# Thirty-two transposes of the identity on TensorE at two places where it waits

## The reference: what is computed

```python
hn = rmsnorm(h_res, norm1_g[l])
proj = hn @ w_in[l]                                  # 1024 x 3072, six groups of 512 columns
qa, ka, va, qb, kb, vb = jnp.split(proj, splits, axis=-1)
...                                                  # two kinds of attention, oa and ob
mix = jnp.concatenate([oa, ob], axis=-1)
h_res = h_res + mix @ w_out[l]
h_res = h_res + peer(rmsnorm(h_res, norm2_g[l]), peer_wq[l], peer_keys[l], peer_u[l], peer_v[l])
```

## Time and profile before

| | us |
|---|---|
| median of 3 runs | 3197.56 |
| lowest, highest | 3196.24, 3198.75 |
| profiled execution, its own time | 3202.24 |
| its span, first to last instruction | 3200.4 |
| mean granted TensorE clock over the span | 0.993 |
| TensorE matmul busy | 3123.5 (98%) |
| TensorE weight load busy | 2822.7 (88%) |

### The profile page before, as it was taken

How to read it: one execution, slowest core, us unless ns; L and a number is a source line. 1 busy time by engine, 2 the same in 40 slices (tenths; PEclk the granted TensorE clock), 3 DMA queues, 4 the chain that set the end, 5 groups by cost and what they waited for, 6 DMA issues and landing times.

```text
span 3200.4 us, 43820 instructions
## 1 busy us (share of the span) xinstructions
PE 3123.5 (98%) x16898; PEld 2822.7 (88%) x16898; DVE 2138.4 (67%) x3594; ACT 1226.4 (38%) x1963; POOL 1709.0 (53%) x843
## 2 busy tenths in 40 slices
PE   8999989999999999999999999988999999999999
PEld 6887888778899999999999999986888888888887
DVE  3512989244485678888888887755776666666665
ACT  4222777221122246666665666642221212122220
POOL 3420000221146665656565666737887877778784
PEclk9999999999999999999999999998999999999999
DMA  4274532312136767777777777997988787878785
GB/s 145 102 237 122 133 80 67 145 66 73 31 122 234 236 213 244 256 256 248 258 246 255 248 259 264 322 356 270 330 301 307 274 304 275 297 276 297 282 290 195
DMA packets 254401, 713.56 MB, mean 223 GB/s; under 512 B 21920, under 2 KB 79904, under 8 KB 247584
## 3 DMA queue, kind: packets, MB, share of 16 engines
q1 hardware_dynamic: 180512, 442.94, 40.8%
q0 software_dynamic: 73728, 268.47, 24.0%
HBM read 577.11 MB, written 134.22 MB: 222 GB/s over the span
## 4 chain that ended last, share of the span: by engine, by line
PE 74%; DMA 4%; POOL 2%; issue 1%; ACT 1%; DVE 1%; SPq 0%; POOLq 0%; ACTq 0%; DVEq 0%
PE banks L2337 30%; PE banks L1506 30%; PE banks L865 5%; PE banks L1519 5%; PE banks L844 3%; DMA score<-in_u,pick_u 2%; PE banks L873 1%; DMA v_raw<-in_v 1%; DMA u_raw<-in_uT 1%; POOL u_lo L1138 1%; DMA gate_in<-gate_d 0%; POOL side_lo L2209 0%; POOL score L1157 0%; DVE score L1429 0%; POOL w_lo L687 0%
## 5 line engine op out<-in xcount | busy, mean ns | idle before, releaser
L1138 POOL TENSOR_TENSOR u_lo<-u_raw,u_hi 128x1024 fp32r<-128x1024 f32 x127 | 357.6, 2816 | 409.8 <-ACT u_hi L1066 409.6
L1506 PE MATMUL banks<-side_hi,u_hi 128*128 128x384 f32 x2048 | 527.9, 338 | 0.0
L1506 PE MATMUL banks<-side_lo,u_hi 128*128 128x384 f32 x2048 | 519.8, 334 | 0.0
L1506 PE MATMUL banks<-side_hi,u_lo 128*128 128x384 f32 x2048 | 519.5, 334 | 0.0
L2337 PE MATMUL banks<-side_hi,act_hi 128*128 128x512 f32 x1488 | 459.9, 390 | 10.8 <-POOL act_lo L2213 6.8
L2337 PE MATMUL banks<-side_lo,act_hi 128*128 128x512 f32 x1488 | 459.6, 390 | 0.0
L2337 PE MATMUL banks<-side_hi,act_lo 128*128 128x512 f32 x1488 | 459.1, 390 | 0.0
L2238 DVE TENSOR_TENSOR acc<-acc,banks 128x1024 f32<-128x1024 f32 x192 | 234.2, 1220 | 332.1 <-PE banks L2337 316.6
L2152 ACT ACTIVATE side_hi<-v_raw 128x2048 fp32r<-128x2048 f32 x62 | 119.0, 1919 | 776.7 <-DMA v_raw<-in_v 472.5
L1506 PEld LDWEIGHTS banks<-side_lo,u_hi 128*128 128x128 f32 x2048 | 370.0, 188 | 0.0
L1506 PEld LDWEIGHTS banks<-side_hi,u_lo 128*128 128x128 f32 x2048 | 369.7, 188 | 0.0
(11 more groups left out here) (250 smaller groups left out, 5645.8 us busy)
## 6 DMA issues: line engine op xcount, KB each, us to landing
u_raw<-in_uT SPq DMA_DIRECT2D x128, 512.0 KB, 3.4
v_raw<-in_v SPq DMA_DIRECT2D x63, 1024.0 KB, 10.1
hid_d<-hid SPq DMA_DIRECT2D x128, 384.0 KB, 5.4
gate_d<-stage SPq DMA_DIRECT2D x48, 1024.0 KB, 8.0
act_in<-hid_d SPq DMA_DIRECT2D x63, 768.0 KB, 8.1
gate_in<-gate_d SPq DMA_DIRECT2D x31, 1536.0 KB, 14.7
w_raw<-in_w_in SPq DMA_DIRECT2D x5, 2048.0 KB, 9.5
k_hi<-k_hi_d SPq DMA_DIRECT2D x32, 256.0 KB, 8.1
```

Of the source, the lines that this page charges most:

```text
L1138: pool.tensor_tensor(u_lo[s % 2][:, :, :], u_raw[:, :, :], u_hi[s % 2][:, :, :].bitcast(F), ALU.subtract).then_inc(u_lo_ok, 1)
L1506: mm = pe.matmul(hid_ps[:, s % 2, half, 0:W], w[s % 2][:, ch], x[:, ch, GB * P + half * W:GB * P + (half + 1) * W], start=n == 0, stop=n = ...
```

## The change

Two loops of 32 instructions are added to TensorE's stream. Each instruction transposes the 128x128 identity, with the identity as the other operand too, into a PSUM place that is written anew before anything reads it. No wait is added, nothing signals anyone, and nothing else is moved.

```diff
             pe.wait_ge(small_in, 32)
+            for n in range(32):
+                pe.transpose(pr_ps[:, 3, 0:P], ident[:, :], ident[:, :])
             for tb in range(TB):
                 turn_x(tb)
...
             last.then_inc(sc_ok, 1)
 
+        for n in range(32):
+            pe.transpose(sc_ps[:, 0, 0], ident[:, :], ident[:, :])
         for g in range(2):
             if g:
                 pe.wait_ge(w_lo_ok, 4)
```

## The result

The changed kernel took 3202.22 us in the median of 22 runs (3198.03 to 3207.07), the kernel before 3197.74 us in 22 runs (3193.53 to 3200.82). The ratio is 1.0014, with a 95% interval of 1.0008 to 1.0020: +4.5 us, between +2.6 and +6.4. That lies within the 0.2% that I had called no change and within the range, but it is four times the +1.1 us of the forecast, which lies outside the interval.

A forecast was written before the change was run, and what follows sets the result against it. TensorE, with an instruction in flight for 98% of the span, was taken to bound the kernel. First place +3.3 and second -2.2 gave +1.1 us on the median 3197.56, so 3198.7 us, range 3194.8 to 3202.8.

The forecast's parts named there:

- The first place: In `project`, before `turn_x(0)`: 32 transposes from 7.0 us delay the chain by 3.3 us, from +2.3 to +6.8.
- the two rows: At the first place: half-clock stretches of 3.5 and 5.9 us, putting the clock's rise at 10.5 or 12.9 us.
- The upper end's 1.9 us: At the first place: clock falling in TensorE's gap and staying down 5.9 us costs 1.9 us more; priced at nothing.
- The second place: In `route`, behind the barrier: 32 transposes keep the clock up for the first item, -2.2 us, from -2.3 to +0.5.
- both shifts reach the end: After both places: later waits up to 1000 us, 6.3 us in all, swallow neither +3.3 nor -2.2 us.
- The sum: Whole kernel: 3.3 - 2.2 = +1.1 us; forecast chance 0.62.
- theory E: Experiments' theory on the first loop: shift costs 3.2 us, the rest of 5.0 comes from the clock state transposes leave.
- The base: Whole kernel: the sum is put on the runs' median, 3197.56 us, not on the profiled execution of 3202.24 us.
- the swallowed case: Past 23 us, something not hanging on TensorE hides the first place's 3.3 us: -2.2, 3195.3 us; chance 0.14.
- transposes don't raise or hold the clock: Both places: 1.2 GHz at the first gives +6.2, lost clock at the second +0.5; +6.7, 3204.3 us; chance 0.10.
- the second place gains nothing: In `route`: the clock falls in another gap nearby or for a reason other than idleness: +3.3, 3200.9 us; chance 0.14.

The follow-up runs named there:

- first_only: Only the first loop of 32 transposes added to the kernel before, no second loop; median 3202.30 us, ratio 1.0017.
- delay_more: No transposes; against the kernel before, ScalarE makes four copies of 128x1024, one of 128x512 and one of 128x320 ahead of its first transposed block's copy; ratio 1.0012.
- before_again: The kernel before, unchanged, run under another name; median 3197.55 us, ratio 1.0000.
- second_only: Only the second loop of 32 transposes added to the kernel before, no first loop; median 3196.23 us, ratio 1.0002.
- second_again: The kernel before with only the second loop of 32, timed once more under another name; median 3196.54 us, ratio 0.9996.
- second_16: The kernel before with only the second loop, cut to 16 transposes instead of 32; median 3197.12 us, ratio 0.9997.
- second_64: The kernel before with only the second loop, lengthened to 64 transposes; median 3199.94 us, ratio 1.0007.
- delay_only: No transposes; against the kernel before, ScalarE makes four copies of 128x1024 and one of 128x512 ahead of its first transposed block's copy; 3200.46 us, ratio 1.0012.
- end_fill: The kernel before with neither loop, but 28 transposes behind the projection's last matmul; median 3197.57 us, ratio 1.0000.

## Why the prediction was right, and where it was off

The outcome, no change that a measurement can tell, and the range came true, and so did the account of both places in the traces. The +1.1 us did not: it lies outside +2.6 to +6.4, and the median ended 0.6 us below the range's upper end. So the hit owes something to a wide range.

**The first place: right.** +3.3 us was forecast. The nine unshifted executions start their attention at 295.33 to 295.57, the changed one and `first_only` at 298.61 and 298.76, so +3.2 to +3.3. The end of the 32 was put at 13.2 and `turn_x(0)` began at 12.71, the transposes counted as work and the full clock came within them. The clock rose at 11.7, between the 10.5 and the 12.9 of the two rows. It fell in the gap behind, which the prediction had priced at nothing because the nearest fall had come after 4 idle us; here 2.7 were enough. The upper end's 1.9 us for it did not come: the spell lasted 3.4 us and not 5.9, and ended behind GpSimd.

**The second place: right in mechanism, too large in size.** -2.2 us was forecast and the mark shows 11.89 - 9.77 = 2.1. But 11.89 is the most that stands there without a loop: the seven executions without one have 11.89, 11.89, 11.75, 11.02, 10.86, 10.79 and 10.68, mean 11.27 (both 11.89 are of the kernel before; the others' code differs ahead of routing). It goes with where the clock falls: 2.6, 2.6 and 2.4 us behind ScalarE's start in the first three, 0.3 to 0.7 behind it, while TensorE is still idle, in the next three; in the last, `delay_more`, it fell late and for 3.4 us instead of 6.8. With a loop of 16 or 32 the mark is 9.75 to 9.79 in all six. Averaged over these traces the loop wins 1.5 us. That is the term that was mis-sized, and in the timed runs even less of it arrives (below).

**Does it last: not shown.** The step "both shifts reach the end" can be followed in the changed kernel to `weigh`'s start, where it is 2.75 us behind `before_again` (2126.99 against 2124.24), which is 1.6 more than the forecast and is the attention's extra spell. From there on executions differ by more than the loops bring: 1071.4 to 1078.7 us.

For the second place the timed runs taken together say more than one ratio. The 32 with the second loop alone (`second_only`, `second_again`, `second_16`) have a mean granted clock of 0.9939, the 66 of the kernel before beside them 0.9931. 0.0008 of 3200 us is about 5 us less at half clock (an estimate: 0.0008 x 3200 x 2), where the traces show a spell of 6.8 us gone. So the loop held the clock in the timed runs too. But their mean time is only 0.3 us lower, between -1.3 and +0.7 by the scatter of the runs. A gain of 2.1, or of 1.5, at the end is not borne out. At `weigh`'s start their three traces still stand at 2121.83 to 2123.60, ahead of the 2124.24 and 2125.41 of the kernel before; what becomes of it behind that, no run shows.

**The sum.** By the traces' terms it is 3.2 - 1.5 = +1.7 us. With what the timed runs give for the second place (-1.3 to +0.7) it is +1.9 to +3.9. The runs say +2.6 to +6.4. The extra spell in the attention costs 1.6 us (275.7 against 274.1), and if it were brought by the change the first sum would be 3.3. But of the six executions whose code and start are the same up to there (before, `before_again`, `second_only`, `second_again`, `second_16`, `second_64`) two have it, and `delay_more` with the same shift has not. So it isn't bound to the change or to the shift; it comes in some executions and not in others. Whether the first loop makes it more frequent is open: one profile for each kernel can't say, and the timed ratios of `first_only` (+2.6 to +8.3) and `delay_more` (+0.6 to +6.7) overlap. The timed runs' clocks give a hint: 0.9922 in `first_only` against 0.9932, which is about 7 us more at half clock (estimated as above), of which the hidden spell at 18.5 is 3.4; the rest is about one more spell. For `delay_only` and `delay_more` together the clock is 0.0002 lower, which their scatter doesn't tell from nothing. That would be theory E, but where in these runs the clock was lost isn't on record. By the traces' terms at least 0.9 us of the measured loss has no shown cause.

**The base.** I put a difference onto the median, which was sound. The profiled execution was 4.7 us above it; 3.4 of its 4.6 us over `before_again` arose in `weigh`, and at both places the two agree to 0.2 us. Compared with the one profile after, it would have made the change look like +0.5.

**The range.** Its lower end of 3194.8 doesn't follow from its own words: the swallowed case is 3195.3, less 1 us 3194.3. Nothing hung on it.

**The rivals.** That transposes don't raise or hold the clock is refuted at both places: the pace of the transposes doubled at 11.7 us, when TensorE had done nothing else, and the clock stood at 1.00 behind them in routing. The Trainium skill's sentence in "TensorE: Matmul & The Clock Gate", Part 4, that the full clock does not engage in transpose mode, does not hold for these float32 transposes. The swallowed shift is refuted by the attention's start. That the second place gains nothing is refuted for the stretch itself, in the traces and by the timed runs' clock. For the whole time it is not: the 32 runs are closer to no gain than to the 2.1 us.

## What to carry to other kernels

Filler work is free only as long as the wait that it fills: at the first place 1.4 us could be filled and 6.1 were, and the engine that looked idle was at the head of a chain through ScalarE and GpSimd back to itself. Behind a barrier with 3.5 us to the first weights, 16 transposes won as much at the mark as 32, so take the fewest that hold the clock. And a term that hangs on where the clock falls needs several executions of the same kernel before it is sized: here one profile's 2.1 was 1.5 on average over the traces, and within 1.3 of nothing in the timed runs. A higher granted clock is not yet a shorter time.

## What the runs showed that I had not expected

The same stretch of the same code meets half clock in some executions and not in others, and how busy TensorE was from 400.9 to 404.1 us doesn't tell which (1.44 us and a fall in `second_16`, 1.46 and none in `second_only`). What does go with it is where the clock fell at the attention's start, over 100 us earlier. The 14 profiled attention blocks fall into two groups by the extra spell: eight of 274.05 to 274.91 us and six of 275.60 to 275.75. Executions differ more in `weigh`, 1071.4 to 1078.7 us to the end; why, no run shows. And holding the clock over a barrier is of no use where the next stretch is thin: in `end_fill` it fell 2.7 us later all the same.
